# The post-norm gate's rows of a two-layer hybrid encoder step: from turns on PE to a round trip through DRAM

## Chip, cores and metric

One NeuronCore of a Trainium2 chip runs the whole step. The metric is the device time in microseconds, as the median of the runs: 1402.86 us for the kernel before (3 runs, 1402.79 to 1405.4). The engines are PE (TensorE), DVE (VectorE), ACT (ScalarE), POOL (GpSimd) and SP (SyncE, which here only issues DMAs). Each engine runs its own program in order and waits on semaphores.

## What is computed

Two layers over 1024 prompt tokens and 64 sample tokens, width 1024, float32. Cut to what matters here:

```python
mod = silu(c) @ w_ada[l] + b_ada[l]               # c_prompt or c_sample: one vector each
shift, scale, gate = split(mod, 3)
h = rms_norm(x, g_pre) * (1.0 + scale) + shift
parts = h @ w_in[l]                               # attention (with an indexer), retention, gates
mixed = concat([o_a * silu(gate_a), o_b * silu(gate_b)])
y = rms_norm(mixed @ w_out[l], g_post[l])
x = x + gate * y                                  # the post-norm gate: gate * g_post, a row of 1024
```

The last line needs, for every token, the row `gate * g_post` along the free dimension. There are four such rows: two layers, times prompt (s = 0) and sample (s = 1).

## The kernel before

**Tiles and stages.** The tokens are nine tiles of 128 rows (`NT` = 9): eight of the prompt, and tile 8 (`SAMPLE`) with 64 rows of the sample, whose low halves lie in the other 64 rows. A layer is ten column chunks in the order `idx`, four times `ret`, `gate`, twice `att`, `OUT0`, `OUT1`, and each chunk is worked through tile by tile. One pair of chunk and tile is a step, 180 in all; `step_of(l, c, t)` numbers them. Every engine walks over the same steps i with four quarters each: PE projects step i + 1 (`project`, three products of 128x512 for each of eight k, as high and low halves) and works in between on the turns, logits and values of earlier steps.

**Products.** `project(g)` writes PSUM bank `proj[g % 2]`, so it waits until ACT has taken step g - 2 (`proj_taken`, in `take_projection`). In the gate chunk ACT evicts the product through Silu to `gate_a[:, t % 2]` (line 1436), and SP stores it to `gates_dram[t]` (line 988); the eviction of tile t waits for the store of tile t - 2 (`gate_stored[t % 2]`).

**Weights.** One slice of 128x512 a step for the next chunk: SP loads it to one of three `w_raw` buffers (`load_raw`, lines 865 to 878), issued two steps ahead, ACT copies its high half (`split_weights`, line 1379), POOL subtracts (`lower_weights`, line 1696). SP's program for a step stands in this order: `w_raw` loads, key stores, `state_out` (line 976), `ret_dram` (line 983), `gates_dram` (line 988), `att_dram` (line 995), gate reads (line 1013), loads of mixed rows (lines 1027 and 1030), store of the new x (line 1041), loads of x for the residual (`load_x`, lines 848 and 850). All of them go through one queue.

**Turns.** Everything that PE transposes goes through `turns`, a ring of two PSUM banks (`RB` = 2) with the order fixed by `plan_units`. PE fills a bank with up to four 128x128 transposes (`turn`, line 1081), another engine takes it. In OUT0, PE turns half of the mixed rows (`mix`) of the tile after next; ACT copies the high halves (lines 1634 and 1637), DVE the low ones (`lower_mixed`, lines 2154 and 2158), and signals `mix_low_ready` with the first of them.

**The gate's rows.** The modulation is computed as columns. `modulate_group` adds them up, and with the last group, in the retention steps of layer 0, DVE signals `mods_ready`: `post_gate[:, l, k, s]` holds `gate * g_post` of feature 128 k + partition, for both layers and both s. `gate_spread(i)` names the steps in which they are made rows: OUT0 tile 5 for s = 0 and tile 6 for s = 1. There PE does for each u in (0, 1) a turn of four columns, each broadcast to 128x128, and ACT copies the bank to `gate_rows[s]` (line 1680), which lies over buffers that the attention used before. So there are 4 x 2 x 4 = 32 transposes and 8 copies. In OUT1, ACT evicts the product to `y1` (OUT0's had gone to `y0`, line 1455) with a sum of squares, POOL makes the root, and DVE's `add_residual` multiplies both halves by root and `gate_rows[s]` (lines 2178 and 2180), adds x (lines 2183 and 2185) and signals `x_new`. SP then stores x and loads the x of a later tile. `mixed[0]` and `mixed[1]` lie in the same part of `score` as tiles 7 and 8 of `y0`.

Of the kernel before, what the change touches and what calls it, by code (L numbers as in the profile page):

```python
# [29 lines left out]
ACT = mybir.ActivationFunctionType  # L30
# [5 lines left out]
P = 128  # L36
# [56 lines left out]
def kind(g):  # L93
    return KIND[lct(g)[1]] if 0 <= g < STEPS else None
# [278 lines left out]
def plan_units():  # L373

    turns, logits = ["vec"], []
    turns += [("h", 0, t, u) for t in (0, 1) for u in (0, 1)]

    for i in range(-1, STEPS + 2):
        j = i - 1
        for q in range(QUARTERS):  # L380
            if q == group_quarter(i) and 0 <= i < STEPS and ada_group(i) is not None:
                turns.append(("ada", ada_group(i)))
            if q == QUARTERS - 1 and mixed_turn(i):
                turns.append(("mix", *mixed_turn(i), 1))
            logits += [("l", j, h, p) for h, p in dots_at(i, q) if dots_unit(j, h, p) == (("l", j, h, p), 0)]
            if kind(j) == "ret" and q == 1:
                logits += [("att", j), ("kv", j)]
            turned = att_head(i, q, TURN_SLOT)
            if turned is not None:
                turns += [("p", *head(turned), p) for p in range(len(att_parts(head(turned)[0])))]  # L390
            if att_step(i, q, BACK_SLOT) is not None:
                turns.append(("o", att_step(i, q, BACK_SLOT)))
            if q == TURN_QUARTER:
                if kind(i) in ("ret", "att"):
                    turns.append(("q", i))
                if has_cache_turn(i):
                    turns.append(("cache", i))
        for lt in hidden_turns(i):
            turns += [("h", *lt, u) for u in (0, 1)]
        if gate_spread(i):  # L400
            turns += [("gg", *gate_spread(i), u) for u in (0, 1)]
    return turns, logits


# [107 lines left out]
def build(nc, x_prompt, x_sample, cache_k_a, cache_v_a, cache_kidx_a, state_s_b, c_prompt, c_sample,  # L512
# [4 lines left out]
    with ExitStack() as ctx:  # L517
# [7 lines left out]
        def sem(name):  # L525
            return ctx.enter_context(nc.semaphore(name))
# [2 lines left out]
        ret_dram = nc.dram_tensor("ret_dram", (NT, P, 512), F32, kind="Internal").ap()  # L529
        att_dram = nc.dram_tensor("att_dram", (NT, P, 512), F32, kind="Internal").ap()  # L530
        gates_dram = nc.dram_tensor("gates_dram", (NT, P, 512), F32, kind="Internal").ap()
        x_dram = nc.dram_tensor("x_dram", (NT, P, D), F32, kind="Internal").ap()


# [128 lines left out]
        x_landed = [sem(f"x_landed{n}") for n in range(3)]  # L663
        mixed_landed = [sem(f"mixed_landed{n}") for n in range(2)]
        gate_landed = [sem(f"gate_landed{n}") for n in range(2)]
        cache_landed = sem("cache_landed")
        vcache_landed = sem("vcache_landed")
        state_landed = sem("state_landed")
# [175 lines left out]
        def _(sp):  # L844
# [75 lines left out]
            for i in range(-1, STEPS + 2):  # L920
# [57 lines left out]
                if roots_ret(i - 1) is not None:  # L978
                    l, c, t = lct(j)
                    sp.wait_ge(ret_out, RET[j] // 3 + 1)  # L980
                    o = RET[j] % 6 - 2
                    a = P * (c - RET0)
                    ret_stores.add(sp.dma_start(ret_dram[t - 2:t + 1, :, a:a + P].rearrange("t p n -> p t n"),
                                                o_raw[:, o:o + 3, :]))
                if kind(i) == "gate":
                    l, c, t = lct(i)
                    sp.wait_ge(proj_taken, i + 1)
                    gate_stores[t % 2].add(sp.dma_start(gates_dram[t], gate_a[:, t % 2, :]))
# [74 lines left out]
        def _(pe):  # L1063
# [228 lines left out]
            for i in range(-1, STEPS + 2):  # L1292
                for q in range(QUARTERS):
                    if i + 1 < STEPS:
                        project(i + 1, q)
                    if q == (2 if kind(i + 1) == "idx" else 1):
                        for a in ada_slices(i + 1):
                            pe.wait_ge(more_landed[a % ADA_SLOTS], 16 * (a // ADA_SLOTS + 1))
                        for a in ada_slices(i + 1):
                            l, grp, k = ADA_LATER[a]  # L1300
                            if k == 0 and a:
                                pe.wait_ge(ada_copied, a // KT)
                            ada(spare, grp, k, ada_more[:, a % ADA_SLOTS, :])
                    if q == group_quarter(i) and 0 <= i < STEPS and ada_group(i) is not None:
                        n = ada_group(i)
                        pe.wait_ge(ada_copied, n + 1)
                        turn(("ada", n), [ada_row(n)[:, b * P:(b + 1) * P] for b in range(4)])
                    if i == -1 and q == 1:
                        turn_hidden(0, 1)
                    if q == 0:  # L1310
                        late(i - 2)
                    if q == QUARTERS - 1 and mixed_turn(i):
                        l, t = mixed_turn(i)
                        pe.wait_ge(mixed_landed[1], 16 * (l * NT + t + 1))
                        turn(("mix", l, t, 1), [mixed[1][:, b * P:(b + 1) * P] for b in range(4)])
                    middle(i - 1, q)
                    if q == TURN_QUARTER and kind(i) in ("idx", "ret", "att"):
                        pe.wait_ge(rope_done, ROPE[i] + 1)
                        src = turned[:, ROPE[i] % 2, :]
                        turn(("q", i), [src[:, 0:P], src[:, P:2 * P]] +  # L1320
                             ([] if kind(i) == "ret" else
                              [src[:, 256:384]]), turns_of(i))
                    if q == TURN_QUARTER and has_cache_turn(i):
                        n = sum(1 for k in range(i + 1) if has_cache_turn(k))
                        pe.wait_ge(cache_landed, 32 * n)
                        turn(("cache", i), [cache_rows[:, b].rearrange("p s e -> p (s e)") for b in range(2)])
                for l, t in hidden_turns(i):
                    turn_hidden(l, t)
                if gate_spread(i):
                    l, s = gate_spread(i)  # L1330
                    pe.wait_ge(mods_ready, 1)
                    for u in (0, 1):
                        key = ("gg", l, s, u)
                        turn(key, [post_gate[:, l, 4 * u + b, s:s + 1].to_broadcast([P, P]) for b in range(4)])


        @block.scalar
        def _(act):
# [51 lines left out]
            def take_projection(g):  # L1390
# [50 lines left out]
                else:  # L1441
                    half = c - OUT0
                    if half == 0:
                        dst = y0[:, t, :]
                        if t == 0:
                            act.wait_ge(neg_ready, heads_through(g - 3))
                    else:
                        dst = y1[t % 2]
                        if t >= 2:
                            act.wait_ge(x_new, l * NT + t - 1)  # L1450
# [168 lines left out]
            for i in range(-1, STEPS + 2):  # L1619
# [46 lines left out]
                if kind(i) == "out" and lct(i)[1] == OUT1 and lct(i)[0] + 1 < DEPTH:  # L1666
                    l, c, t = lct(i)
                    if t < SAMPLE:
                        act.wait_ge(x_new, l * NT + t + 1)
                        square_x(x_ordinal(l, t))  # L1670
                if gate_spread(i):
                    l, s = gate_spread(i)
                    if s == 0:
                        turns.wait_taken(act, ("o", ATT_STEPS[(l + 1) * NKV * NT - 1]))
                        act.wait_ge(att_stored[0], 16 * NT * (l + 1))
                        act.wait_ge(att_stored[1], 16 * NT * (l + 1))
                    for u in (0, 1):
                        key = ("gg", l, s, u)
                        turns.wait_full(act, key)
                        turns.take(nc.scalar.activation(gate_rows[s][:, u * 512:(u + 1) * 512], turns.bank(key)[:],  # L1680
                                                        ACT.Copy), key)
                if 4 <= i + 5 < NT:
                    t = i + 5
                    wait_x(act, t)
# [114 lines left out]
        def _(dve):  # L1799
# [368 lines left out]
            def add_residual(l, t, unit, parts=(0, 1)):  # L2168
# [3 lines left out]
                x, row, y = xt(n), gate_rows[s], y1[t % 2]  # L2172
                if 0 in parts:
                    dve.wait_ge(proj_taken, step_of(l, OUT1, t) + 1)
                    turns.wait_taken(dve, ("gg", l, s, 0))
                    turns.wait_taken(dve, ("gg", l, s, 1))
                    dve.wait_ge(rstd_ready, unit + 1)
                    do(nc.vector.scalar_tensor_tensor(y0[:, t, :], y0[:, t, :], root(unit, 0), row[:, 0:512],
                                                      ALU.mult, ALU.mult))
                    do(nc.vector.scalar_tensor_tensor(y, y, root(unit, 0), row[:, 512:1024], ALU.mult, ALU.mult))  # L2180
                    wait_x(dve, n)
                    fence()
                    do(nc.vector.tensor_tensor(x[:, 0:512], x[:, 0:512], y0[:, t, :], ALU.add))
# [204 lines left out]
```

## Time and profile before

| what | value |
|---|---|
| median of 3 runs | 1402.86 us |
| profiled execution, its own time | 1403.68 us |
| its span | 1401.8 us |
| busy: PE weight loads / DVE / ACT / POOL | 75% / 73% / 55% / 29% |
| mean granted clock of TensorE | 0.994 |
| DMA: read and written | 93.02 MB, 26.64 MB |
| `mods_ready` signalled by DVE (line 2224) | 269.3 us |
| gate chunk of layer 0, first and last eviction | 376.89 and 422.23 us |
| first and last gate turn, layer 0 | 664.5 and 672.3 us |
| last gate turn, layer 1 | 1341.5 us |

A page of the profile gives the busy time of each engine, the span in 40 slices, the DMA queues, the chain of work that ended last, the costliest groups and the DMA issues. The trace below it gives the same for any stretch, instruction by instruction. Times are us from the start of the span. Matmul ends are modelled and overlap, so the price of work on PE is read from starts. "issue" is time in which an engine waited for nothing that the profile shows.

### The profile page before, as it was taken

What the parts mean: (1) busy time and instruction counts of PE and PEld (TensorE: products, weight loads), DVE (VectorE), ACT (ScalarE), POOL (GpSimd) and SP (SyncE); (2) the same over time, 40 slices, a digit from 0 to 9 for tenths busy, and PEclk for the clock granted to TensorE, in tenths of its full rate; (3) what the DMA queues carried; (4) which work ended last, traced back from release to release, by engine and by line L of the source; (5) the groups of instructions that cost most, each with busy time, mean ns of one, the idle gap of its engine ahead of it and who ended that gap; (6) DMA issues with size and microseconds to landing.
All of it is one profiled execution on the core that took longest, in us unless ns stands there. A gap on an engine that the chain in (4) does not pass through costs nothing.

```text
span 1401.8 us, 24971 instructions
## 1 busy us (share of the span) xinstructions
PE 1351.7 (96%) x7883; PEld 1057.9 (75%) x7883; DVE 1029.6 (73%) x3043; ACT 774.2 (55%) x1894; POOL 405.1 (29%) x382
## 2 busy tenths in 40 slices
PE   6999999999999999999998999999999999999997
PEld 2865777788888778777877577878788877876786
DVE  0686999999998656652398789999999866565225
ACT  2545666666415675674454566666642467567422
POOL 3741324434431001001387114433443100100100
PEclk9999999999999999999999999999999999999999
DMA  8743343112132112214252111211213211222325
GB/s 307 241 123 121 93 135 112 55 52 63 49 90 67 43 47 72 67 61 124 94 183 69 42 34 36 53 48 52 63 31 94 78 43 36 72 73 67 116 84 171
DMA packets 126537, 121.29 MB, mean 87 GB/s; under 512 B 35369, under 2 KB 95625, under 8 KB 126409
## 3 DMA queue, kind: packets, MB, share of 16 engines
q1 hardware_dynamic: 125952, 119.58, 28.5%
q8 instruction: 66, 1.08, 0.3%
q14 instruction: 63, 0.51, 0.1%
q10 hardware_dynamic: 456, 0.13, 0.0%
HBM read 93.02 MB, written 26.64 MB: 85 GB/s over the span
## 4 chain that ended last, share of the span: by engine, by line
PE 53%; DVE 34%; issue 5%; POOL 2%; DMA 2%; ACT 2%; DVEq 0%; ACTq 0%; SPq 0%; POOLq 0%
DVE U L1924 12%; PE proj L1104 10%; PE proj L1105 9%; PE proj L1107 9%; PE turn L1081 8%; PE out_bank L1188 5%; PE logit L1158 3%; PE logit L1137 3%; DVE turned L1879 2%; DVE by_cos_sin L1864 2%; PE spare L1158 2%; DVE probsT_more L1997 2%; DVE by_cos_sin L1862 2%; DVE probsT_more L2001 1%; POOL h_lo L1702 1%
## 5 line engine op out<-in xcount | busy, mean ns | idle before, releaser
L1104 PE MATMUL proj<-w_hi,h_hi 128*128 128x512 f32 (+2 forms) x1440 | 575.7, 400 | 1.2 <-POOL h_hi L1702 0.6
L1105 PE MATMUL proj<-w_lo,h_hi 128*128 128x512 f32 (+2 forms) x1440 | 536.4, 373 | 0.0
L1107 PE MATMUL proj<-w_hi,h_lo 128*128 128x512 f32 (+2 forms) x1280 | 478.4, 374 | 0.0
L1696 POOL TENSOR_TENSOR w_lo<-w_raw,w_hi 128x512 fp32r<-128x512 f32 (+2 forms) x160 | 202.2, 1265 | 714.3 <-ACT w_hi L1379 713.9
L1104 PEld LDWEIGHTS proj<-w_hi,h_hi 128*128 128x128 f32 x1440 | 272.8, 189 | 52.4 <-issue 17.2
L1105 PEld LDWEIGHTS proj<-w_lo,h_hi 128*128 128x128 f32 x1440 | 273.1, 190 | 31.2
L1107 PEld LDWEIGHTS proj<-w_hi,h_lo 128*128 128x128 f32 x1280 | 241.2, 188 | 37.2
L1924 DVE TENSOR_SCALAR_CACHE_REDUCE U<-score,cand 128x384 bf16<-128x384 f32 x310 | 223.0, 752 | 2.2
L1523 ACT ACTIVATE probsT_more<-turn 128x384 f32<-128x384 f32 (+3 forms) x150 | 73.3, 492 | 87.1 <-PE turn L1081 86.3
L1379 ACT ACTIVATE w_hi<-w_raw 128x512 fp32r<-128x512 f32 (+2 forms) x160 | 95.0, 595 | 12.2 <-DMA w_raw<-in_w_in_dram 12.1
L1712 POOL TENSOR_TENSOR rstd<-means,minus_half 128x3 f32<-128x3 f32 (+2 forms) x42 | 32.2, 766 | 215.4 <-DVE means L2052 148.6
L1557 ACT ACTIVATE U<-U,neg_max 128x384 f32<-128x384 f32 (+7 forms) x102 | 78.0, 764 | 20.6 <-DVE neg_max L2080 20.1
L1081 PE MATMUL turn<-ident,U 128*128 128x128 f32 x514 | 84.7, 282 | 3.1 <-DVE U L2144 1.9
L1081 PEld LDWEIGHTS turn<-ident,U 128*128 128x128 f32 x514 | 58.0, 140 | 34.2 <-issue 21.9
L1576 ACT ACTIVATE U<-score,cand 128x896 bf16<-128x896 f32 x62 | 64.7, 1043 | 34.2 <-DVE cand L1962 34.2
L1879 DVE TENSOR_TENSOR turned<-by_cos_sin 128x256 f32<-128x256 f32 (+1 forms) x126 | 73.7, 585 | 10.1 <-DVE by_cos_sin L1864 0.5
L2071 DVE CUSTOM_DVE_ANT_0 U<-logit,score 128x512 f32<-128x512 f32 (+3 forms) x70 | 38.6, 560 | 52.8 <-PE logit L1158 52.2
L1188 PE MATMUL out_bank<-probsT_more,U 128*64 128x256 f32 (+1 forms) x468 | 72.6, 377 | 0.0
L1576 ACT ACTIVATE probsT_more<-score,cand 128x1024 bf16<-128x1024 f32 x62 | 70.5, 1136 | 0.0
L1723 POOL TENSOR_SCALAR U<-U,probs_last,rstd 128x128 f32<-128x128 f32 x72 | 64.7, 908 | 0.0
L1544 ACT ACTIVATE U<-logit 128x512 f32<-128x512 f32 (+4 forms) x66 | 32.9, 533 | 56.4 <-PE logit L1137 56.2
L1862 DVE TENSOR_TENSOR by_cos_sin<-rows,cos_b 128x256 f32<-128x256 f32 (+1 forms) x108 | 50.5, 468 | 12.0 <-ACT rows L1440 8.6
(230 smaller groups left out, 2290.4 us busy)
## 6 DMA issues: line engine op xcount, KB each, us to landing
w_raw<-in_w_in_dram SPq DMA_DIRECT2D x80, 256.0 KB, 3.3
probsT_more<-in_w_ada_dram SPq DMA_DIRECT2D x64, 256.0 KB, 3.8
score<-in_w_ada_dram SPq DMA_DIRECT2D x32, 256.0 KB, 4.9
w_raw<-in_w_out_dram SPq DMA_DIRECT2D x32, 256.0 KB, 3.1
U<-in_x_prompt_dram SPq DMA_DIRECT2D x12, 512.0 KB, 4.3
ret_dram<-U SPq DMA_DIRECT2D x24, 192.0 KB, 2.1
gates_dram<-U SPq DMA_DIRECT2D x18, 256.0 KB, 2.1
score<-ret_dram SPq DMA_DIRECT2D x18, 256.0 KB, 3.0
```

The source lines that it names most:

```text
L1081: ins = nc.tensor.transpose(ring.bank(key)[:, n * P:(n + 1) * P], piece, ident[:])
L1104: nc.tensor.matmul(out, h_hi[:, k, tile], hi, start=(k == 0), stop=False)
L1105: ins = nc.tensor.matmul(out, h_hi[:, k, tile], lo, start=False, stop=(t == SAMPLE and k == KT - 1))
L1107: ins = nc.tensor.matmul(out, h_lo[:, k, tile], hi, start=False, stop=(k == KT - 1))
L1188: ins = nc.tensor.matmul(out_bank[HD * pair:HD * pair + HD, 0:P * heads_of(g) // 2], v, p_, start=(kb == 0), stop=(kb == nblk - 1))
L1379: nc.scalar.activation(w_hi[:, s % WS, 0:w], w_raw[:, n % RAWS, 0:w], ACT.Copy).then_inc(w_hi_ready, 1)
L1557: nc.scalar.activation(probs[n % 4][:, 0:w], probs[n % 4][:, 0:w], ACT.Exp, bias=neg_max[:, n % 4:n % 4 + 1], scale=ATT_SCALE, accum_out=r ...
L1576: nc.scalar.activation(tested[n % 2][:, 0:valid_keys(t)], scores(t)[:, 0:valid_keys(t)], ACT.Sign, bias=cand[:, col:col + 1].bitcast(F32) ...
L1696: nc.gpsimd.tensor_tensor(w_lo[:, s % WS, 0:w], w_raw[:, n % RAWS, 0:w], w_hi[:, s % WS, 0:w].bitcast(F32), ALU.subtract).then_inc(w_lo_re ...
L1862: do(nc.vector.tensor_tensor(by_cos[:, 0:w].rearrange("p (h n) -> p h n", n=half), src.rearrange("p (h n) -> p h n", n=half), cs, ALU.mult))
L1879: signal(nc.vector.tensor_tensor(turned[:, ro % 2, 0:w], by_cos[:, 0:w], by_sin[:, 0:w], ALU.add), rope_done, ro + 1)
L1924: ins = nc.vector.tensor_scalar(found[:, n % 2, 0:valid_keys(t)], s, cand[:, j:j + 1].bitcast(F32) if b else 0.0, extra(t), ALU.is_ge, ALU ...
```

## The change

- SP, in the first gate step of layer 0: wait for `mods_ready`, then four stores (two layers, two s) of the columns `post_gate[:, l, :, s]` to a new DRAM tensor `post_gate_dram[l, s]`, each 128 partitions x 8 floats to a row of 1024. They stand ahead of the `gates_dram` store of that step.
- SP, in the steps of `gate_spread`: wait until the four have landed, until the last attention turn of the layer is taken and the `att_dram` stores have landed, then one load of `post_gate_dram[l, s]`, broadcast to all 128 partitions, into `gate_rows[s]` (512 KB).
- PE loses the 32 transposes, ACT the eight copies with their waits; the ring's plan loses the units `gg`.
- DVE's `add_residual` waits for the layer's two loads in place of the turns.
- ACT, before it evicts tile 7 of OUT0 to `y0`, waits for the last `mix_low_ready` of the layer.

```diff
--- before.py
+++ after.py
@@ -397,8 +397,6 @@
                     turns.append(("cache", i))
         for lt in hidden_turns(i):
             turns += [("h", *lt, u) for u in (0, 1)]
-        if gate_spread(i):
-            turns += [("gg", *gate_spread(i), u) for u in (0, 1)]
     return turns, logits
 
 
@@ -529,6 +527,7 @@
         ret_dram = nc.dram_tensor("ret_dram", (NT, P, 512), F32, kind="Internal").ap()
         att_dram = nc.dram_tensor("att_dram", (NT, P, 512), F32, kind="Internal").ap()
         gates_dram = nc.dram_tensor("gates_dram", (NT, P, 512), F32, kind="Internal").ap()
+        post_gate_dram = nc.dram_tensor("post_gate_dram", (DEPTH, 2, D), F32, kind="Internal").ap()
         x_dram = nc.dram_tensor("x_dram", (NT, P, D), F32, kind="Internal").ap()
 
 
@@ -663,6 +662,8 @@
         x_landed = [sem(f"x_landed{n}") for n in range(3)]
         mixed_landed = [sem(f"mixed_landed{n}") for n in range(2)]
         gate_landed = [sem(f"gate_landed{n}") for n in range(2)]
+        gates_kept = sem("gates_kept")
+        gate_rows_landed = sem("gate_rows_landed")
         cache_landed = sem("cache_landed")
         vcache_landed = sem("vcache_landed")
         state_landed = sem("state_landed")
@@ -982,6 +983,20 @@
                     a = P * (c - RET0)
                     ret_stores.add(sp.dma_start(ret_dram[t - 2:t + 1, :, a:a + P].rearrange("t p n -> p t n"),
                                                 o_raw[:, o:o + 3, :]))
+                if i == step_of(0, GATE, 0):
+                    sp.wait_ge(mods_ready, 1)
+                    for l in range(DEPTH):
+                        for s in (0, 1):
+                            sp.dma_start(post_gate_dram[l, s].rearrange("(k p) -> p k", p=P), post_gate[:, l, :, s], allow_slow_non_contiguous=True)\
+                              .then_inc(gates_kept, 16)
+                if gate_spread(i):
+                    l, s = gate_spread(i)
+                    sp.wait_ge(gates_kept, 16 * 2 * DEPTH)
+                    turns.wait_taken(sp, ("o", ATT_STEPS[(l + 1) * NKV * NT - 1]))
+                    for st in att_stores:
+                        st.wait(sp)
+                    sp.dma_start(gate_rows[s], post_gate_dram[l, s:s + 1, :].to_broadcast([P, D]))\
+                      .then_inc(gate_rows_landed, 16)
                 if kind(i) == "gate":
                     l, c, t = lct(i)
                     sp.wait_ge(proj_taken, i + 1)
@@ -1326,12 +1341,6 @@
                         turn(("cache", i), [cache_rows[:, b].rearrange("p s e -> p (s e)") for b in range(2)])
                 for l, t in hidden_turns(i):
                     turn_hidden(l, t)
-                if gate_spread(i):
-                    l, s = gate_spread(i)
-                    pe.wait_ge(mods_ready, 1)
-                    for u in (0, 1):
-                        key = ("gg", l, s, u)
-                        turn(key, [post_gate[:, l, 4 * u + b, s:s + 1].to_broadcast([P, P]) for b in range(4)])
 
 
         @block.scalar
@@ -1444,6 +1453,8 @@
                         dst = y0[:, t, :]
                         if t == 0:
                             act.wait_ge(neg_ready, heads_through(g - 3))
+                        if t == SAMPLE - 1:
+                            act.wait_ge(mix_low_ready, l * NT + NT)
                     else:
                         dst = y1[t % 2]
                         if t >= 2:
@@ -1668,17 +1679,6 @@
                     if t < SAMPLE:
                         act.wait_ge(x_new, l * NT + t + 1)
                         square_x(x_ordinal(l, t))
-                if gate_spread(i):
-                    l, s = gate_spread(i)
-                    if s == 0:
-                        turns.wait_taken(act, ("o", ATT_STEPS[(l + 1) * NKV * NT - 1]))
-                        act.wait_ge(att_stored[0], 16 * NT * (l + 1))
-                        act.wait_ge(att_stored[1], 16 * NT * (l + 1))
-                    for u in (0, 1):
-                        key = ("gg", l, s, u)
-                        turns.wait_full(act, key)
-                        turns.take(nc.scalar.activation(gate_rows[s][:, u * 512:(u + 1) * 512], turns.bank(key)[:],
-                                                        ACT.Copy), key)
                 if 4 <= i + 5 < NT:
                     t = i + 5
                     wait_x(act, t)
@@ -2172,8 +2172,7 @@
                 x, row, y = xt(n), gate_rows[s], y1[t % 2]
                 if 0 in parts:
                     dve.wait_ge(proj_taken, step_of(l, OUT1, t) + 1)
-                    turns.wait_taken(dve, ("gg", l, s, 0))
-                    turns.wait_taken(dve, ("gg", l, s, 1))
+                    dve.wait_ge(gate_rows_landed, 16 * (2 * l + 2))
                     dve.wait_ge(rstd_ready, unit + 1)
                     do(nc.vector.scalar_tensor_tensor(y0[:, t, :], y0[:, t, :], root(unit, 0), row[:, 0:512],
                                                       ALU.mult, ALU.mult))
```

## Rows read from the trace of the kernel before

**Rows 1.** The page, busy us (share of the span) of each engine.

```profile
PE 1351.7 (96%) x7883; PEld 1057.9 (75%) x7883; DVE 1029.6 (73%) x3043; ACT 774.2 (55%) x1894; POOL 405.1 (29%) x382
```

**Rows 2.** Timeline of PE, layer 0: start us, us, line, operation [idle before].

```profile
658.11 0.60 PE L1081 MATMUL turn<-ident,score 128*128 128x128 f32 x4
658.46 0.48 PE L1104 MATMUL proj<-w_hi,h_hi 128*128 128x512 f32 x1
...
664.04 0.60 PE L1081 MATMUL turn<-ident,score 128*128 128x128 f32 x4
...
665.57 0.65 PE L1081 MATMUL turn<-ident,post_gate 128*128 128x128 f32 x4 [0.50 <-DVE h_hi L2158]
665.98 0.47 PE L1104 MATMUL proj<-w_hi,h_hi 128*128 128x512 f32 x1
...
671.54 1.03 PE L1081 MATMUL turn<-ident,post_gate 128*128 128x128 f32 x8
672.33 0.47 PE L1104 MATMUL proj<-w_hi,h_hi 128*128 128x512 f32 x1
672.65 0.39 PE L1105 MATMUL proj<-w_lo,h_hi 128*128 128x512 f32 x1
672.87 0.39 PE L1104 MATMUL proj<-w_hi,h_hi 128*128 128x512 f32 x1
```

**Rows 3.** Timeline of PE at the same places of layer 1.

```profile
1333.26 0.60 PE L1081 MATMUL turn<-ident,score 128*128 128x128 f32 x4
...
1335.20 0.48 PE L1104 MATMUL proj<-w_hi,h_hi 128*128 128x512 f32 x1
...
1340.76 1.03 PE L1081 MATMUL turn<-ident,post_gate 128*128 128x128 f32 x8
1341.55 0.47 PE L1104 MATMUL proj<-w_hi,h_hi 128*128 128x512 f32 x1
1341.86 0.39 PE L1105 MATMUL proj<-w_lo,h_hi 128*128 128x512 f32 x1
```

**Rows 4.** Waits of PE, 1320 us to the end: us, times, longest.

```profile
PE turn L1081 <- DVE h_hi L2158: 0.5, 1, 0.5
```

**Rows 5.** Chain that ended last, 590 to 810 us: start, us, what.

```profile
671.71 0.87 PE turn L1081 x8
...
683.87 1.25 DVE score L2178
...
687.65 4.47 DMA U<-in_x_prompt_dram
```

**Rows 6.** Groups by line: busy us, mean ns, idle before.

```profile
L1680 ACT ACTIVATE U<-turn 128x512 f32<-128x512 f32 x4 | 2.2, 615 | 0.0
```

**Rows 7.** Timeline of SP: issues at the two additions' places.

```profile
382.60 0.43 SPq L988 DMA_DIRECT2D gates_dram<-U  x1
...
659.58 3.07 SPq L865 DMA_DIRECT2D w_raw<-in_w_in_dram  x2
```

**Rows 8.** Timeline of ACT: evictions of gate tiles 2 and 3.

```profile
389.17 0.60 ACT L1436 ACTIVATE U<-proj 128x512 f32<-128x512 f32 x1 [3.73 <-PE proj L1107]
...
394.61 0.60 ACT L1436 ACTIVATE U<-proj 128x512 f32<-128x512 f32 x1 [4.43 <-PE proj L1107]
```

**Rows 9.** DMA issues: count, KB each, median us to landing.

```profile
U<-in_x_prompt_dram SPq DMA_DIRECT2D x12, 512.0 KB, 4.3
ret_dram<-U SPq DMA_DIRECT2D x24, 192.0 KB, 2.1
gates_dram<-U SPq DMA_DIRECT2D x18, 256.0 KB, 2.1
...
out_dram<-U SPq DMA_DIRECT2D x32, 32.0 KB, 1.5
```

**Rows 10.** Timelines of ACT and DVE as layer 0's attention begins.

```profile
424.30 0.43 ACT L1440 ACTIVATE rows<-proj 128x320 f32<-128x320 f32 x1
...
425.39 1.30 DVE L1862 TENSOR_TENSOR by_cos_sin<-rows,cos_b 128x320 f32<-128x320 f32 x1
```

## Prediction

> **What bounds the kernel now.** I read the page's busy times first. PE is busy for 1351.7 of 1401.8 us [rows 1], so time that is taken off PE's order is worth having wherever PE itself is what the rest waits for, and nothing where PE waits for DVE. The second view is PE's timeline at the two places of the change. In layer 0 the products of the projection start every 0.22 us (672.65 to 672.87), and the gate's turns stand between them in PE's order [rows 2]; layer 1 repeats the picture [rows 3]. The third is the list of who waited for whom on PE from 1320 us to the end: one wait of 0.5 us, and that one is for a gate turn itself (it needs the PSUM bank that DVE's `lower_mixed` is still reading) [rows 4]. From the gate's turns of layer 1 to its last product PE is never late. The fourth is the chain that ended last: the eight turns at 671.71 lie on it, and it goes on through the first residual (DVE at 683.87) into a series of residual loads, one of them a DMA of 4.47 us at 687.65 [rows 5]. So in layer 0 too the turns are on the path, but what follows them is handed to DVE and DMA.
>
> **What is removed: 32 turns.** By the mean duration of a transpose these would seem large, but the durations on PE overlap: eight turns take 1.03 us together, and the next product starts 0.79 us after the first of them [rows 2]. The price must be read from starts.
> - Layer 0, the prompt's row, eight turns behind the four of the mixed row. Where the mixed row's turns stand alone, the next product starts 0.35 us after them (658.11 to 658.46). With the gate's, it starts 1.94 us after them (664.04 to 665.98). The difference is 1.59 us, with the 0.50 us wait for DVE's read of the bank in it [rows 2].
> - Layer 0, the sample's row, eight turns between two products: 671.54 to 672.33 is 0.79 us, and the product behind a turn is followed after 0.32 us in place of 0.22 or 0.23 (672.33 to 672.65), so 0.88 us [rows 2].
> - Layer 1: 1333.26 to 1335.20 is again 1.94, less 0.35 is 1.59; 1340.76 to 1341.55 is 0.79, and 0.31 in place of 0.23 behind it, so 0.87 [rows 3].
>
> Sum: 1.59 + 0.88 + 1.59 + 0.87 = 4.93 us.
>
> **The eight copies on ACT** are about 0.61 us each [rows 6]. In these steps ACT is done early and then waits for PE's product, so I put them at nothing beyond the turns; PE did not wait for them in layer 1 [rows 4].
>
> **Is the gain kept?** In layer 1, yes: PE has no other wait to the end. In layer 0 the residual at 683.87 waits for PE's first product of OUT1, which comes 2.47 us earlier, and each load of the series waits for the residual and the store before it. Nothing in that series is tied to anything but PE's start, so I let the whole series move, and the search of layer 1 behind it.
>
> **What is added: four stores of single floats.** They are issued once, by SP, in the first gate step of layer 0, after the wait for `mods_ready` (its group of the modulation was finished in the retention steps, long before) and ahead of that step's `gates_dram` store, which SP issued at 382.60 [rows 7]. `post_gate[:, l, :, s]` has its floats two apart in SBUF and 128 apart in DRAM, so each store is 1024 runs of 4 B, 4096 in all. No row shows such a store. Queued behind them are the store of gate tile 0, the `w_raw` slices 3 and 4 of the next chunk and the store of gate tile 1. I call X the time for which the four hold the queue.
> - Who waits: ACT's eviction of gate tile 2 needs tile 0 stored (same half of `gate_a`); before, it ran at 389.17. PE's tile 4 needs that eviction, and starts when PE is through with tile 3, at about 394.6, where ACT takes it [rows 8]. The eviction takes 0.6 us, so the store must land by 394.0, that is 11.4 us after 382.60. The store itself takes 2.1 us [rows 9]. PE is not held up while X is at most 9.3 us. A second path, through `w_raw` slice 3, ACT's split, POOL's `lower_weights`, POOL's `gate_retained` and the `ret_dram` store to the store of gate tile 2, I judge to be about as tight.
> - What a delay of PE costs there: DVE is working without a gap on the masks and takes the first rotation of the attention at 425.39. Its rows begin to be copied at 424.30 and take 0.43 us, so PE has 0.66 us to spare [rows 10]. A stall therefore costs X - 9.3 - 0.7, or X less 10.0 us, and nothing below.
> - Size of X from the nearest rows: `ret_dram<-U`, 384 runs of 512 B, lands in 2.1 us; `out_dram<-U` of 32 KB, 128 runs of 256 B, in 1.5 us [rows 9]. That is 0.6 us for 256 more runs, 2.3 ns a run, and 4096 x 2.3 ns = 9.6 us. The low end: if a run costs by its bytes, the four are no more than a small store each, 1.5 us, and they overlap: X under 6 us, and no gain from it. The high end: if a 4 B run costs twice a 512 B one, 19.2 us. I take 9.6, since both rows are stores to DRAM with short runs, and their difference in landing lies with the number of runs. Cost in the sum: 0.
> - The Trainium skill, page "DMA: Bandwidth & Descriptors", section "Rules for kernel authors", says that a non-contiguous last dimension becomes one descriptor for each element, and its section "Specifications" that transfers below 512 B bring a read-modify-write. The first agrees with my count of runs; the second no row here shows, since the 256 B runs landed faster than the 512 B ones. By the second rule the rival below would be the forecast.
>
> **What is added: two loads a layer.** Each reads one 4 KB row 128 times, 512 KB. The nearest row is the 512 KB load of x, 4.3 us [rows 9]. SP issues them where it runs freely, next to the `w_raw` loads of 659.58 [rows 7]; two take under 10 us even one after the other, and they are first read by DVE at 683.87 [rows 5]. The idle queue and 24 us hide them; if a load that reads one place took twice as long, 8.6 us each, both would still be there in time. Their waits on the last attention turn and the `att_dram` stores are met: SP has passed the same stores for the mixed rows. Cost 0.
>
> **What is added: ACT's wait** for the last `lower_mixed` before it evicts tile 7 of OUT0. DVE does that step at about the 0.50 us wait of [rows 2], one whole projection before the eviction. Behind the wait would stand the eviction and PE's tile after next, but it is met. DVE's `gate_rows_landed` in place of two turn waits: also met. Cost 0.
>
> **Sum.** 1403.68 us (profiled run; span 1401.8) less 4.93 is 1398.75. The median of the runs is 0.82 us lower, 1402.86, which gives 1397.93. I forecast 1397.9 us, 0.35% faster.
>
> **Rivals.**
> - *The stores hold the queue.* X doubles to 19.2 us, because each small write costs more than its place in the queue: the stall is 9.2 us, and the time 1402.86 - 4.93 + 9.2 = 1407.1, slower. It decides from X = 10.0 + 4.93 = 14.9 us, 3.6 ns a run, and counts as slower by 0.2% from X = 17.7, 4.3 ns. For it: the room for the queue (9.3 us) is hardly the forecast X; nothing like 4 B runs is in the trace. Against it: the run rate of the nearest stores, and that DVE is the bound just there. Chance 0.22.
> - *Little is left.* Either X is 12 to 17 us, so 2 to 7 of the 4.93 are given back (1400 to 1405), or layer 0's 2.47 us get lost in the residual loads and only layer 1's 2.46 stay: 1400.4. For the second: DMA steps of 4.5 us are on the chain from 687 on [rows 5]. Against: the series starts at PE's product. Chance 0.20.
> - *The change doesn't do what it says*, as its loads come late and the first residual waits: needs a load of over 10 us. Under 0.02, kept in the case before.
>
> **How the numbers follow.** 0.58 for the forecast, 0.20 and 0.22 for the others. About 0.2%, 2.8 us, is what a measurement of this kernel can tell from no change. Range: the forecast's own is 1396 to 1400, down by one or two us should a wait behind the turns shrink as well. To leave out no more than 2 in 10 it must take in the middle case and the smaller half of the slower one, up to 1407. I give 1395.8 to 1407.
>
> **What would show it.** No `turn<-post_gate`; PE's product follows the mixed row's turns after 0.35 us at the place of 664.04, and nothing stands at 671.54. The store of gate tile 0 lands about 12 us after the first small store is issued; ACT's eviction of tile 2 waits for a DMA; PE has at most a gap of some tenths ahead of tile 4. DVE's first rotation of the attention stays within 0.5 us of 425.39, and PE's OUT1 of layer 0 starts 2.5 us earlier against that. I am wrong if PE has a wait of several us between 390 and 410, or if the small stores land later than 15 us after their issue.

## The result, and the profile after

The changed kernel takes 1411.72 us (median of 4, 1410.14 to 1412.58) against 1403.74 us of before (4 runs): slower, ratio 1.0057, 95% interval 1.0045 to 1.0069. The prediction was 1397.9 us with a range up to 1407, so it was wrong in sign and in range. The profiled run of after took 1411.96 us with a span of 1410.2; before's took 1403.68 with 1401.8.

The page of after: busy times, the shares of the chain that ended last, and the costliest group of PE (busy us, mean ns, then idle before and its releaser).

```profile
PE 1345.7 (95%) x7851; PEld 1052.1 (75%) x7851; DVE 1026.8 (73%) x3043; ACT 769.2 (55%) x1886; POOL 405.2 (29%) x382
...
PE 55%; DVE 30%; issue 5%; DMA 4%; POOL 3%; ACT 2%; DVEq 0%; SPq 0%; ACTq 0%; POOLq 0%
...
L1119 PE MATMUL proj<-w_hi,h_hi 128*128 128x512 f32 (+2 forms) x1440 | 575.6, 400 | 14.7 <-ACT U L1445 11.8
```

The new DMA issues of after (count, KB each, median us to landing):

```profile
probsT_more<-post_gate_dram SPq DMA_DIRECT2D x2, 512.0 KB, 6.8
post_gate_dram<-post_gate SPq DMA_DIRECT2D x4, 4.0 KB, 17.3
```

PE is busy for 6.0 us less than in [rows 1], and one wait leads its idle time that was not there before: 11.8 us ahead of a product, ended by ACT's eviction of a gate tile. The 4 KB stores take a median of 17.3 us to land. The place, in the timelines of SP, ACT and PE of after (start us, us, operation, idle before):

```profile
382.07 2.31 SPq L990 DMA_DIRECT2D post_gate_dram<-post_gate  x4
384.43 0.58 SPq L1003 DMA_DIRECT2D gates_dram<-U  x1
...
405.16 0.60 ACT L1445 ACTIVATE U<-proj 128x512 f32<-128x512 f32 x1 [20.23 <-DMA gates_dram<-U]
...
393.67 0.39 PE L1122 MATMUL proj<-w_hi,h_lo 128*128 128x512 f32 x1
405.81 0.79 PE L1119 MATMUL proj<-w_hi,h_hi 128*128 128x512 f32 x1 [11.76 <-ACT U L1445]
406.41 0.63 PE L1120 MATMUL proj<-w_lo,h_hi 128*128 128x512 f32 x1
406.83 0.63 PE L1122 MATMUL proj<-w_hi,h_lo 128*128 128x512 f32 x1
```

The store of gate tile 0, which in [rows 9] landed 2.1 us after its issue, is issued at 384.43 behind the four small ones and lands 20.7 us later. ACT's eviction of gate tile 2, at 389.17 in [rows 8], runs at 405.16, and PE waits 11.76 us for it ahead of gate tile 4. Then PE goes on at half speed: its products start 0.43 us apart (406.41 to 406.83) where they had started 0.23 apart. The stretches of after (us in all, busy us of PE, PE's weight loads, DVE, ACT and POOL, then PE's granted clock, the busy share of the DMA engines, GB/s):

```profile
394.00:398.00 4.00, 0.06 (x1) 0.00 (x0) 3.86 (x8) 0.00 (x0) 0.00 (x0) 1.00 0.80 14
398.00:406.00 8.00, 0.19 (x1) 0.19 (x2) 7.79 (x10) 0.78 (x2) 0.00 (x0) 0.51 0.94 98
406.00:411.00 5.00, 5.00 (x12) 3.94 (x13) 4.89 (x7) 1.35 (x3) 4.58 (x3) 0.50 0.01 2
411.00:416.00 5.00, 5.00 (x22) 4.02 (x22) 4.90 (x7) 0.00 (x0) 3.72 (x4) 0.93 0.27 85
```

The clock falls to its lower level (1.2 of 2.4 GHz) some 4 us into PE's idle time and is back at about 411.5. Of the 5.7 us that PE works in that stretch about half, 2.8 us, is lost.

The turns' places came out as forecast. PE of after, where the gate's turns had stood behind the mixed row's in [rows 2]:

```profile
677.51 0.60 PE L1096 MATMUL turn<-ident,score 128*128 128x128 f32 x4
677.87 0.48 PE L1119 MATMUL proj<-w_hi,h_hi 128*128 128x512 f32 x1
```

The next product starts 0.36 us after the turns, in place of 1.94.

**Where the 8.4 us of the span came from**, by the same instruction in both traces. ACT's first gate eviction, at 376.89 before, is at 376.38 (-0.5). ACT's rows of the first attention tile, at 424.30 in [rows 10], come at 438.62: +14.3, so the gate chunk lost 14.8 us, which is the wait of 11.8 and the slow clock's 2.8 but for 0.2. DVE's first rotation, at 425.39 in [rows 10], is at 439.08: +13.7, so 0.6 us were taken up there, the 0.66 that the prediction gave PE to spare. SP's load of the mixed row before the last turns, issued at 657.01 before, is at 670.49: +13.5. SP's first store of x, 687.21 before, is at 698.19: +11.0, so OUT0 of layer 0 gained 2.5. PE's turns of the mixed row ahead of the same place in layer 1, at 1333.26 in [rows 3], are at 1343.92: +10.7. The end is at +8.4, so layer 1 gained 2.3 behind them.

### The profile page after: what moved, and what is told of

It reads as the page before. It is cut to its first block, busy times and chain, and to the rows that moved or that the text cites. A ratio compares the mean times of both kernels' runs of the same rounds, so it can differ in the third digit from the quotient of the medians.

```text
span 1410.2 us, 24891 instructions
## 1 busy us (share of the span) xinstructions
PE 1345.7 (95%) x7851; PEld 1052.1 (75%) x7851; DVE 1026.8 (73%) x3043; ACT 769.2 (55%) x1886; POOL 405.2 (29%) x382
## 4 chain that ended last, share of the span: by engine, by line
PE 55%; DVE 30%; issue 5%; DMA 4%; POOL 3%; ACT 2%; DVEq 0%; SPq 0%; ACTq 0%; POOLq 0%
DVE U L1924 12%; PE proj L1119 11%; PE proj L1120 10%; PE proj L1122 10%; PE turn L1096 8%; PE out_bank L1203 5%; PE logit L1173 3%; PE logit L1152 3%; DVE turned L1879 2%; DVE by_cos_sin L1864 2%; PE spare L1173 2%; DVE by_cos_sin L1862 2%; DMA gates_dram<-U 1%; POOL h_lo L1702 1%; DVE probsT_more L1997 1%
## 5 line engine op out<-in xcount | busy, mean ns | idle before, releaser
L1119 PE MATMUL proj<-w_hi,h_hi 128*128 128x512 f32 (+2 forms) x1440 | 575.6, 400 | 14.7 <-ACT U L1445 11.8
L1388 ACT ACTIVATE w_hi<-w_raw 128x512 fp32r<-128x512 f32 (+2 forms) x160 | 94.8, 594 | 12.3 <-DMA w_raw<-in_w_in_dram 12.2
```

The costliest lines, as they stand in the source:

```text
L1119: nc.tensor.matmul(out, h_hi[:, k, tile], hi, start=(k == 0), stop=False)
L1388: nc.scalar.activation(w_hi[:, s % WS, 0:w], w_raw[:, n % RAWS, 0:w], ACT.Copy).then_inc(w_hi_ready, 1)
```

## Experiments

Theory after the result: all of the loss is in the four small stores, which hold the way of other DMAs for 21 us in place of 9.6, and the turns' gain is real. The questions were whether the loads or ACT's new wait take a part, whether SP's queue or the DMA engines are held, whether another place would do, and what makes such a store dear.

**The stores alone** (`stores_only`), on the kernel before:

```diff
+                if i == step_of(0, GATE, 0):
+                    sp.wait_ge(mods_ready, 1)
+                    for l in range(DEPTH):
+                        for s in (0, 1):
+                            sp.dma_start(post_gate_dram[l, s].rearrange("(k p) -> p k", p=P), post_gate[:, l, :, s], allow_slow_non_contiguous=True)\
+                              .then_inc(gates_kept, 16)
                 if kind(i) == "gate":
...
+            sp.wait_ge(gates_kept, 16 * 2 * DEPTH)
```

> The kernel before with nothing but the four small stores added at the place of the change; the turns and copies stay. Theory: it costs what the changed kernel lost and the turns' gain besides, 8.0 + 4.9 = 12.9 us: about 1416.6, with a wait of PE of about 12 us ahead of gate tile 4. Rival (the turns bring nothing): about 1411.7, the same as the changed kernel. Rival (the loss comes from the loads): 1403.7.

1416.25 us against 1403.52, ratio 1.0090 (1.0076 to 1.0104): 12.7 us slower. Waits of PE, 370 to 440 us (us, times, longest):

```profile
PE proj L1113 <- ACT U L1445: 11.6, 1, 11.6
```

The wait of the changed kernel is all there without its loads, and 12.7 less the 8.0 of the change leaves 4.7 us for the turns. Neither rival fits: they had 1411.7 and 1403.7.

**The columns turned once** (`one_turn`), on the changed kernel. In place of the four stores (the edit in short, not as code):

```diff
+PE, end of gate tile 2's step:  for l: transpose(bank[0:16], post_gate[:, l] as 128x16)
+ACT, the same step:             for l: vec[32 * l:32 * l + 16, :] = bank[0:16]
+SP, the next step:              for l, s: dma(post_gate_dram[l, s] as (8, 128), vec[32 * l + s:32 * l + 16:2, :])
```

> The changed kernel, but the columns are turned once by PE (two transposes of 128x16 in gate tile 2 of layer 0, two copies of 16x128 by ACT) and stored as four DMAs of 8 runs of 512 B. The two broadcast loads a layer, DVE's and ACT's waits are as in the change. Theory (all of the loss is the small writes, the turns' price of 4.9 us is real and nothing else costs): no wait of PE over 1 us in the gate chunk, 4.9 less 0.3 for the two transposes: 1398.9 against 1403.5 of before, ratio 0.9967. Rival (the loads or ACT's new wait take part of it back): 1401 to 1403.5.

1398.27 us against 1404.12, ratio 0.9958 (0.9944 to 0.9971): 5.9 us faster than before, and 13.8 faster than the change, each against the runs of before beside it. The store is of 32 runs of 512 B in all. PE has no wait for ACT or a DMA in the gate chunk, so the loads and ACT's new wait cost nothing that shows. It is the version that beats both kernels. PE of this kernel does the two transposes at once. The third product behind them starts at 395.79; without them, at one start each 0.227 us from 394.88, it would be 395.56, so they cost 0.2 us. ACT does the two copies:

```profile
394.88 0.39 PE L1125 MATMUL proj<-w_hi,h_lo 128*128 128x512 f32 x1
395.11 0.38 PE L1351 MATMUL turn<-ident,post_gate 128*16 128x128 f32 x2
395.25 0.48 PE L1122 MATMUL proj<-w_hi,h_hi 128*128 128x512 f32 x1
395.56 0.40 PE L1123 MATMUL proj<-w_lo,h_hi 128*128 128x512 f32 x1
395.79 0.39 PE L1125 MATMUL proj<-w_hi,h_lo 128*128 128x512 f32 x1
...
395.80 0.54 ACT L1694 ACTIVATE vec<-turn 16x128 f32<-16x128 f32 x2
```

**Runs of 32 B** (`runs_32`), on the changed kernel; the same 4 KB a store, contiguous on both sides. The gate's values then stand in another order, so this kernel leaves out the right result and serves for its time alone:

```diff
-post_gate_dram[l, s].rearrange("(k p) -> p k", p=P), post_gate[:, l, :, s]
+post_gate_dram[l, s].rearrange("(p k) -> p k", p=P), post_gate[:, l, 4 * s:4 * s + 4, :].rearrange("p k s -> p (k s)")
```

> The changed kernel with the four stores at the place of the change, each of 4 KB as before, but contiguous on both sides: 128 runs of 32 B in place of 1024 of 4 B. The rows then hold the gate's values in another order, so y is not the reference's; nothing else is changed. Theory (the price is in the 4 B writes): the four land within 3 us of their issue, PE does not wait in the gate chunk, 1398.6. Rival (any store below 512 B is slow here): 128 runs in place of 1024 cost an eighth, 2.7 us for the four, and PE does not wait either; it is told apart by the landing, above 2.5 us for each alone.

1398.44 us against 1404.12, ratio 0.9962 (0.9948 to 0.9975). Each of the four lands 1.5 us after its issue. Same place, same number of bytes, same number of DMAs: the 8.0 us of loss have become a gain of 5.7.

**Through ACT's queue** (`stores_act`), on the changed kernel: the same four stores as `act.dma_start`, in ACT's program of the same step.

> The changed kernel with the four small stores issued by ACT, through its own queue, in the same gate step; ACT is idle there. Theory in its first form (the order within SP's queue is what holds up the gate tile's store): the store of gate tile 0 no longer stands behind them, lands in about 2 to 4 us, PE does not wait, about 1398.8. Rival (the 16 DMA engines themselves are held by the small writes, whatever the queue): the store of gate tile 0 still lands after about 20 us and the time stays near 1411.

1406.66 us against 1403.52, ratio 1.0020 (1.0011 to 1.0029). The timelines with the issues of both queues and ACT's eviction of gate tile 2, and then the stretch from 380 to 390 us (last two columns: DMA share, GB/s):

```profile
377.74 2.85 ACTq L1660 DMA_DIRECT2D post_gate_dram<-post_gate  x4
381.61 0.43 SPq L997 DMA_DIRECT2D gates_dram<-U  x1
...
400.50 0.60 ACT L1439 ACTIVATE U<-proj 128x512 f32<-128x512 f32 x1 [9.40 <-DMA gates_dram<-U]
```

```profile
380.00:390.00 10.00, 10.00 (x47) 8.34 (x47) 6.46 (x14) 0.60 (x1) 0.00 (x0) 1.00 2.07 6
```

The first form of the theory is wrong. Gate tile 0's store has none of the four before it in SP's queue, and still lands 18.8 us after its issue. In those 10 us the DMA engines show as occupied twice over (a share of 2.07, packets overlap) while they move 6 GB/s; before, they moved 115 GB/s in the same stretch at a share of 0.41. So what is held is something that both queues share, the engines or the way behind them. The run is 5 us faster than the change, and 4.2 of that is PE's wait, 7.6 us in place of 11.8, as ACT issues 4.3 us earlier. Here ACT also waits 7.4 us for a weight slice and copies the retention late, for which DVE waits 4.4.

**Spread in the gate chunk** (`stores_spread`), on the changed kernel: one store in each step of gate tiles 2 to 5.

> The changed kernel, but the four small stores are issued one a step in gate tiles 2 to 5 of layer 0 in place of all four in tile 0. Theory (the four together hold SP's queue for about 22 us and hold up the store of gate tile 0): one store holds the queue about 5.5 us, which the gate steps of 5.4 us with their slack of one step absorb, PE has no wait over 1 us between 380 and 440 us, and the turns' 4.9 us are gained: about 1398.8 against 1403.7 of before. Rival (the loss sits in the two broadcast loads, or in ACT's new wait, in OUT0): still slower than before, about 1411. Rival (the turns' place is refilled by other waits): PE has no wait in the gate chunk, and the time is within 1 us of before.

A miss: 1410.49 us against 1403.52, ratio 1.0049 (1.0035 to 1.0063). The stores land after 11.8, 19.0, 22.1 and 21.5 us, the last at 432.2, so the four take 36.5 us from the first issue, more than the 22 us when issued together. PE has four waits in place of one. Waits of ACT and PE, 390 to 440 us:

```profile
ACT U L1444 <- DMA gates_dram<-U: 29.1, 4, 13.4
...
PE proj L1118 <- ACT U L1444: 9.3, 4, 4.2
ACT w_hi L1387 <- DMA w_raw<-in_w_in_dram: 5.8, 2, 3.6
```

They land 9.5, 8.5 and 6.7 us apart, not 5.5, and a gate step is 5.4: they pile up.

**Apart in the retention chunks** (`stores_apart`), on the changed kernel: one store in each of the steps 32, 36, 40, 44.

> The changed kernel, but the four small stores are issued one at a time in steps 32, 36, 40 and 44, in the retention chunks ahead of the gate chunk of layer 0, where SP issues in bursts some 19 us apart. Theory (a lone small store holds the DMA engines for about 9 us; in the retention chunk a weight slice has more than that to spare): no wait of PE over 1 us, about 1398.8. Rival (each store costs its hold wherever it stands): PE waits for w_hi or w_lo after each of them, 1404 to 1412.

A miss too: 1408.79 us against 1404.12, ratio 1.0035 (1.0023 to 1.0048), though the four stores land 10 to 12.5 us after their issues, which are 20 us or more apart. Waits of DVE and ACT, 300 to 425 us:

```profile
DVE probs_last L2045 <- ACT U L1596: 6.5, 2, 4.9
...
ACT w_hi L1387 <- DMA w_raw<-in_w_in_dram: 15.0, 3, 8.1
```

ACT waits for weight slices in order and comes late with the retention's copy, on which DVE waits 6.5 us. Before, DVE had no wait from 300 to 425 us: it is the bound there. Not all of this is the retention chunks' doing. The fourth store is issued at 384.73, when the gate chunk has begun (its first eviction is at 382.88), and behind it stand 4.9 of DVE's 6.5 us, at 398, and a wait of PE of 3.2 us for a gate tile. By the places in both traces, the gate chunk begins 6.0 us late (382.88 for 376.89) after three stores, and the attention rows come 9.4 us late (433.73 for 424.30), so the fourth costs 3.4. DVE's listed waits up to 380 us are 2.5 us in sum, so how three stores come to 6.0 is not fully followed. In both chunks there is less room than the far-apart issues suggest.

**Five kinds of store in the gate chunk** (`probe_kinds`), on the kernel before:

> The kernel before with one extra store to scratch DRAM in each of gate tiles 2 to 6 of layer 0, of five kinds of 4 KB each, in this order: (1) as in the change, 4 B runs, neighbours in DRAM come from different partitions; (2) 4 B runs from the same places, but each partition's eight floats lie together in DRAM; (3) 4 B runs, each to a place of its own 512 B apart; (4) source contiguous in SBUF, destination as in (1); (5) both contiguous, 128 runs of 32 B. Theory A (the count of runs sets the price): (1) to (4) land after the same 6 to 8 us, (5) after 1.5 us. Theory B (writes of different partitions to the same stretch of DRAM get into each other's way): (1) and (4) 6 to 8 us, (2) and (3) 3 to 4 us, (5) 1.5 us. The time stays within 3 us of before.

Landings after issue: 11.8, 21.0, 17.8, 18.6 and 10.4 us. They overlapped, so only their order of landing tells something: kind (3), a float every 512 B, landed 2.3 us behind (2), and (5) 1.5 us behind (4), where (2) and (4) each took 8 us or more. The time of 1415.49 us is a single one, and with 12 us over before it is far from the 3 expected. Inconclusive as a price, and the reason for the next.

**Each kind alone** (`probe_alone`): eleven DMAs behind all work of the kernel before, each waited for, in one execution.

> The kernel before with eleven DMAs behind all its work, each waited for before the next is issued, so that each landing is that of one DMA alone: 4 KB as 1024 runs of 4 B (1) as in the change; (2) each partition's eight floats side by side in DRAM; (3) a float every 32 B; (4) every 64 B; (5) every 512 B; (6) contiguous in SBUF, places in DRAM as in (1); (7) 128 runs of 32 B; (8) 384 runs of 512 B; (9) the change's load of one 4 KB row to 128 partitions; (10) a load of 512 KB of x; (11) as (1) again. Theory B (writes that fall in the same stretch of DRAM hold each other up; the run count does not matter much): (1), (2), (6) and (11) about 10 us, (5) 2 to 4 us, (3) and (4) between, (7) and (8) about 2 us. Theory A (run count): (1) to (6) all about 10 us. (9) 5 to 7 us against 4 for (10) if one row read 128 times is slower, the same if not.

| DMA alone | us to landing |
|---|---|
| (1) as in the change, 1024 runs of 4 B; (11) again | 8.9; 10.5 |
| (2) a partition's eight floats side by side in DRAM | 7.7 |
| (3) a float every 32 B | 3.0 |
| (4) a float every 64 B | 2.5 |
| (5) a float every 512 B | 2.4 |
| (6) contiguous in SBUF, places in DRAM as (1) | 11.3 |
| (7) 128 runs of 32 B | 1.4 |
| (8) 384 runs of 512 B | 1.9 |
| (9) one 4 KB row to 128 partitions | 3.7 |
| (10) 512 KB of x, by the next issue | 3.2 |

The answers of the trace for (1), (3) and (7), each for the one instruction that starts there:

```profile
L1075 SPq DMA_DIRECT2D probe_dram<-post_gate x1: 378/378/378, 1401.0 to 1401.0; - x1
...
DMA to landing us min/median/max: 8.9/8.9/8.9
...
L1075 SPq DMA_DIRECT2D probe_dram<-post_gate x1: 372/372/372, 1417.6 to 1417.6; - x1
...
DMA to landing us min/median/max: 3.0/3.0/3.0
...
L1075 SPq DMA_DIRECT2D probe_dram<-post_gate x1: 332/332/332, 1436.8 to 1436.8; - x1
...
DMA to landing us min/median/max: 1.4/1.4/1.4
```

From (7) to (5), 896 more runs cost 1.0 us, 1.1 ns each; the run count is cheap even at 4 B. With the places 32 B apart it is 1.8 ns. With eight of them in the same 32 B, from eight partitions or from one, it is 7 to 11 ns. The theory of the run count falls; what is dear is 4 B writes packed side by side in DRAM. The two stretches of (1) and of (3), to the last packet of the DMA engines and from there to the landing (columns as above; DMA share and GB/s last), show where:

```profile
1401.90:1402.70 0.80, 0.00 (x0) 0.00 (x0) 0.00 (x0) 0.00 (x0) 0.00 (x0) 0.50 0.60 5
1402.70:1409.90 7.20, 0.00 (x0) 0.00 (x0) 0.00 (x0) 0.00 (x0) 0.00 (x0) 0.50 0.00 0
1418.40:1419.30 0.90, 0.00 (x0) 0.00 (x0) 0.00 (x0) 0.00 (x0) 0.00 (x0) 0.50 0.53 5
1419.30:1420.60 1.30, 0.00 (x0) 0.00 (x0) 0.00 (x0) 0.00 (x0) 0.00 (x0) 0.50 0.00 0
```

The engines' own packets are over in less than 1 us for both. After that they show no work, and the packed store lands 7.2 us later, the spaced one 1.3. So by the trace the price arises behind the engines' packets, and no busy time of an engine tells it when the store is alone.

**The same at the place of the change** (`spaced_32b`): `stores_only` with one float every 32 B.

```diff
-sp.dma_start(post_gate_dram[l, s].rearrange("(k p) -> p k", p=P), post_gate[:, l, :, s], ...)
+sp.dma_start(post_gate_dram[l, s].rearrange("(k p n) -> p k n", p=P, n=8)[:, :, 0], post_gate[:, l, :, s], ...)
```

> The kernel before with four small stores at the place of the change, as in stores_only, of the same 1024 runs of 4 B each and from the same places in SBUF; only their places in DRAM differ, one float every 32 B in place of eight in 32 B. Theory (the runs that fall into the same 32 B hold each other up; a lone store took 3.0 us spaced and 8.9 to 11.3 packed): the four hold the engines for 6 to 8 us, the store of gate tile 0 lands within 11 us of the first store's issue, PE does not wait: within 1 us of before. Rival (the number of runs on a busy queue sets the price): as stores_only, 12.7 us slower than before.

1402.29 us against 1403.58, ratio 0.9992 (0.9983 to 1.0001): the 12.7 us are gone with nothing changed but the spacing, and with it the stretch of DRAM that each store covers. SP's stores, and their landings:

```profile
L991 SPq DMA_DIRECT2D post_gate_dram<-post_gate x4: 433/576/584, 381.8 to 383.6; - x4
...
DMA to landing us min/median/max: 3.0/5.5/7.3
```

The store of gate tile 0 behind them lands at 391.0, 9.2 us after the first issue.

**One packed store** (`one_store_b`): `stores_only` with the row of l = s = 0 alone.

> The kernel before with one of the four packed stores at the place of the change. The prediction's threshold was a hold of 9.3 us before PE waits and 10.0 before it costs. A first store landed 10.3 to 10.8 us after its issue, so the gate tile's store should land about 12 us after it: a wait of PE of 0 to 1.5 us and 0 to 1 us slower than before. Rival (the threshold is wrong and the cost goes with the number of stores): a quarter of 12.7 us, 3.2 us slower.

1403.95 us against 1403.58, ratio 1.0002 (0.9992 to 1.0011). It lands after 12.3 us, the gate store behind it at 395.3, and PE waits (us, times, longest):

```profile
PE proj L1113 <- ACT U L1445: 1.6, 1, 1.6
```

So the cost is not a fixed share a store (3.2 us would be a quarter of 12.7, and the interval ends at 1.5): it begins where the prediction had put the threshold.

## Why the prediction was wrong, point by point

- **The turns' price, 4.93 us: right.** `stores_only` against the change gives 4.7, the landmarks of the trace 2.5 and 2.3 in the two layers, `one_turn` 5.9 (4.1 to 7.9 by the ends of its interval), `runs_32` 5.7. The size is known to 1 or 2 us. The reading by starts was the right one.
- **The gain of layer 0 is kept through the residual loads: right.** +13.5 before the place, +11.0 behind it, and still +10.7 at the place in layer 1.
- **The room before PE waits, 9.3 us: right.** X, from the first small store's issue to the landing of gate tile 0's store less the 2.1 us of that, is 384.43 + 20.7 - 382.07 - 2.1 = 21.0 us in the changed kernel. X less 9.3 is 11.7, and PE waited 11.76. With one store, issued at 382.4, X is 395.3 - 382.4 - 2.1 = 10.8, less 9.3 is 1.5, and PE waited 1.6; with the spaced ones X is 7.1 and PE didn't wait. The second path, through POOL, did not come first in the changed kernel: PE's only wait in that chunk is the one of 11.76.
- **The size of X: the step that failed.** It was 9.6 us by 2.3 ns a run (2.34; with 2.3 it is 9.4), from the difference in landing of two stores to DRAM [rows 9]. In those every run fills 256 or 512 B; the step took the number of runs as the only thing that matters. For runs 32 B apart that was near: X of the spaced stores is 7.1 us, 1.7 ns a run. The packed ones took 21.0, 5.1 ns a run on the mean, and not evenly, as a single store already makes X 10.8. My high end had been 19.2 and was too low as well, so the range fell short.
- **The rival with its price** (the stores hold the queue, 1407.1 us by X = 19.2) had the right wait, at a chance of 0.22; its reason, that each small write is dear, was not the right one, as the same writes 32 B apart are cheap. It fell short of 1411.7 by X, and by a term that the sum had not: after 11.8 us without work PE's clock ran at half for the next 5.7 us of products, 2.8 us. With X = 21.0 and that, the sum is 1403.74 - 4.93 + 11.0 + 2.8 = 1412.6. Its words "hold the queue" were wrong too: `stores_act` shows that a store of another queue is held as well.
- **The two loads at nothing: right.** They landed in 5.5 and 6.8 us (medians), ahead of their use; alone, such a load takes 3.7 us against 3.2 for x.
- **ACT's wait and DVE's wait at nothing: right**, as far as `one_turn` has them both and gains in full.
- The Trainium skill, page "DMA: Bandwidth & Descriptors", section "Specifications", asks for transfers of 512 B or more for the full rate of the line, with a read-modify-write below. No run here measures a rate. As a price of a 4 KB store it does not show: 128 runs of 32 B land in 1.4 us, less than 384 runs of 512 B in 1.9, and 1024 runs of 4 B in 3.0 when they lie 32 B apart. As a warning of this change it was still of more use than my extrapolation.

What stays open: why packed stores issued together land 2 to 5 us apart, and interleaved with other DMAs 7 to 10. The mechanism behind the engines is not shown. Nor is its unit: places 4 B apart are dear and places 32 B apart are not, but none in between was run, and the spaced store also spreads over 32 KB of DRAM in place of 4. Whether the writes that share 32 B matter, or the number of writes into a short stretch, no run here tells apart.

## What to carry to other kernels

Before a transposed store of single floats is put on a queue, look at how its writes lie in DRAM (here eight in each 32 B), not only at the number of its runs, and price it by a store that does the same; if there is none, its price is unknown upwards. Here it was 2.2 times the guess. One transpose a layer of all columns on PE, followed by stores of whole 512 B runs, cost 0.2 us of PE's order here and gave the full gain. These stores were in the way of the other queue too, so moving them to another engine's queue moved only their start.

## What the runs showed of the hardware that I had not expected

- 1024 writes of 4 B to DRAM, to landing, each alone: 8.9 to 11.3 us when eight from eight partitions lie in 32 B, 7.7 us when the eight come from one partition, 3.0 us at one per 32 B, 2.4 us at one per 512 B. Being contiguous in SBUF (11.3 us) did not help.
- Of the 8.9 us the DMA engines show packets for less than 1 us; the other 7.2 they show none.
- Four such stores delay a 256 KB store of another queue as they do one of their own: 18.8 and 20.7 us to landing in place of 2.1.
- Four of them behind each other took 22 us from the first issue to the last landing, four with other DMAs between them 36.5 us.
- PE's granted clock went to half about 4 us after PE had run dry and stayed there for some 6 us of work; in `one_store_b`, with a wait of 1.6 us, it stayed at full.
